# A transformer layer on one core: gate/up as seven block products, tokens in two groups

## The reference

```
n  = rms_norm(x, norm_mix_g)
h  = x + concat(window_attention(n), diff_attention(n)) @ w_out
m  = rms_norm(h, norm_ffn_g)
y  = h + (silu(m @ w_gate) * (m @ w_up)) @ w_down
return rms_norm(y, final_norm_g), keys and values
```

## Time and profile before

| | us |
|---|---|
| runs (3), median | 2766.35 |
| lowest and highest | 2764.15 to 2767.64 |
| span of the profiled execution | 2764.0 |
| TensorE busy | 2640.0 |
| VectorE busy | 1581.0 |
| ScalarE busy | 1136.4 |
| GpSimd busy | 444.8 |
| DMA queues, mean | 48 GB/s |

### The profile page before, as it was taken

One profiled execution on the slowest core, in us unless ns is written; L12 is line 12 of the kernel. 1 busy time (PEld: TensorE's weight loads), 2 busy tenths in 40 slices (PEclk: granted clock), 3 DMA queues, 4 the chain that ended last, 5 costly groups with the idle time before them and its releaser, 6 DMA issues.

```text
span 2764.0 us, 48120 instructions
## 1 busy us (share of the span) xinstructions
PE 2640.0 (96%) x19852; PEld 1645.9 (60%) x19852; DVE 1581.0 (57%) x3263; ACT 1136.4 (41%) x2090; POOL 444.8 (16%) x530
## 2 busy tenths in 40 slices
PE   3999999978899998999999999999999999999998
PEld 1666666656667766555656565656565555656564
DVE  8777776768888773665462525353444444353516
ACT  4566666657889997544211111111120111111113
POOL 1211111105667666000000000000000000000001
PEclk9999999988999999999999999999999999999999
DMA  4123211142210000521101101010101010101003
GB/s 184 54 74 109 93 57 65 46 107 51 40 32 9 9 9 17 190 92 61 54 8 46 31 16 31 16 39 9 39 8 46 1 47 1 46 1 47 1 8 126
DMA packets 119197, 132.95 MB, mean 48 GB/s; under 512 B 42642, under 2 KB 97346, under 8 KB 117954
## 3 DMA queue, kind: packets, MB, share of 16 engines
q1 hardware_dynamic: 118978, 129.87, 14.8%
HBM read 92.20 MB, written 34.84 MB: 46 GB/s over the span
## 4 chain that ended last, share of the span: by engine, by line
PE 58%; DVE 1%; DMA 1%; ACT 0%; issue 0%; POOL 0%; POOLq 0%; ACTq 0%
PE y_ps L2325 6%; PE y_ps L2327 6%; PE y_ps L2326 6%; PE hnT_ps L2312 6%; PE hnT_ps L2313 6%; PE hnT_ps L2314 6%; PE mixT_ps L2312 6%; PE mixT_ps L2313 6%; PE mixT_ps L2314 6%; PE y_ps L2297 2%; PE y_ps L2299 2%; PE y_ps L2298 2%; DMA tail_buffers<-mix_scratch 1%; PE mixT_ps L2274 1%; PE hnT_ps L2284 0%; DVE tail_buffers L2054 0%
## 5 line engine op out<-in xcount | busy, mean ns | idle before, releaser
L2079 DVE SCALAR_TENSOR_TENSOR residual_rows<-y_ps,pair_scales,residual_rows 128x512 f32<-128x512 f32 (+1 forms) x374 | 276.8, 747 | 101.4 <-PE y_ps L2327 100.5
L2312 PE MATMUL hnT_ps<-ffn_inT_hi,tail_buffers 128*128 128x352 f16 x1056 | 330.0, 313 | 0.7 <-ACT ffn_inT_hi L2184 0.7
L2312 PE MATMUL mixT_ps<-ffn_inT_hi,tail_buffers 128*128 128x352 f16 x1056 | 330.1, 313 | 0.0
L2313 PE MATMUL hnT_ps<-ffn_inT_lo,tail_buffers 128*128 128x352 f16 x1056 | 330.0, 313 | 0.0
L2313 PE MATMUL mixT_ps<-ffn_inT_lo,tail_buffers 128*128 128x352 f16 x1056 | 330.0, 313 | 0.0
L2314 PE MATMUL hnT_ps<-ffn_inT_hi,tail_buffers 128*128 128x352 f16 x1056 | 330.0, 313 | 0.0
L2314 PE MATMUL mixT_ps<-ffn_inT_hi,tail_buffers 128*128 128x352 f16 x1056 | 330.0, 313 | 0.0
L2213 ACT ACTIVATE w_out_halves<-mixT_ps,pair_scales 128x352 f32<-128x352 f32 x66 | 36.6, 554 | 706.2 <-PE mixT_ps L2314 706.2
L1094 PE MATMUL z_ps<-w_in_hi_lo,normT_hi 128*128 128x384 f16 x816 | 268.5, 329 | 21.8 <-DVE w_in_hi_lo L681 21.8
L2067 DVE SCALAR_TENSOR_TENSOR w_out_halves<-hnT_ps,pair_scales,w_out_halves 128x352 f32<-128x352 f32 x66 | 38.5, 584 | 432.6 <-ACT w_out_halves L2213 432.6
L2325 PE MATMUL y_ps<-w_out_halves 128*128 128x512 f16 (+1 forms) x748 | 283.8, 379 | 0.0
(11 more groups left out here) (317 smaller groups left out, 5385.0 us busy)
## 6 DMA issues: line engine op xcount, KB each, us to landing
tail_buffers<-in_w_gate SPq DMA_DIRECT2D x11, 1024.0 KB, 5.4
tail_buffers<-in_w_up SPq DMA_DIRECT2D x11, 1024.0 KB, 8.0
tail_buffers<-in_w_down SPq DMA_DIRECT2D x22, 512.0 KB, 3.2
keys_values<-in_w_in SPq DMA_DIRECT2D x8, 1152.0 KB, 16.0
x_tile<-in_x SPq DMA_DIRECT2D x17, 512.0 KB, 3.7
tail_buffers<-mix_scratch SPq DMA_DIRECT2D x17, 512.0 KB, 3.7
residual_rows<-in_x SPq DMA_DIRECT2D x17, 512.0 KB, 4.6
out_y_prompt<-tail_buffers SPq DMA_DIRECT2D x16, 512.0 KB, 2.6
```

The costliest lines, as they stand in the source:

```text
L2079: nc.vector.scalar_tensor_tensor(out, YP[(2 * t + n) % 4][0:rows, :], PS[0:rows, i, F_YI:F_YI + 1], out, ALU.mult, ALU.add).then_inc(h_ok, 1)
L2312: nc.tensor.matmul(out, FH[w][:, k, c], nh, start=k == 0, stop=False)
L2313: nc.tensor.matmul(out, FH[w][:, k, c], nl, start=False, stop=False)
```

## The change

It touches `phase_output_ffn` (and one small transfer in the first stage, a row copy of the norm gain). What it does:

- **Block products.** The gate and up products of a pair are taken as 2 x 2 block products: the width 1024 in two halves of 512, the tokens in two halves. Seven products of blocks and sums of blocks stand for the eight (a scheme of Strassen with sums reused). `PRODUCTS`, `PSUM_OF` and `SLOT_AT` are its tables: which token block or sum a product reads, which PSUM bank it goes to, and where its weight slot lies. Per matrix x (0 gate, 1 up) three banks are used, 0 to 2 and 3 to 5; the down products use 0, 1, 6 and 7. j counts the seven products.
- **Token sums.** The normed rows of two tiles, one of each token half, make four sums (`token_sums`, GpSimd), and 28 chunks in place of 16 are split (`row_hi`, `row_lo`) and transposed (`turn`, in four batches, 56 transposes for two tiles).
- **Weight sums.** GpSimd makes four sums of weight blocks for each pair (`weight_sums`), ScalarE and VectorE split seven slots of 1024 elements (`slot_hi`, `slot_lo`).
- **Sums of products.** ScalarE copies the first product out (`copy_1`), VectorE forms `sum_2`, `sum_3`, `block_22`, `block_21`, `block_12`, and four activations follow in place of two for a block.
- **Two groups of tokens.** The first group has 8 tiles (1024 tokens, halves of 512), the second 9 (1088 tokens, halves of 544, run as 256 and 288 columns). Output tiles 0 to 8 in the order `ORDER`, then 11 pairs, then output tiles 9 to 16, then 11 pairs again. The weight halves made in the first group are stored to DRAM scratch (`store_slot`, `store_down`) and loaded in the second (`slot_back`, `down_back`). Residual rows are kept for 9 tiles and reused.

The core of the diff:

```diff
-NTOK = SEQ + DEC
-TB = 6
-TBW = NTOK // TB
+ORDER = (0, 4, 1, 5, 2, 6, 3, 7, 16, 8, 12, 9, 13, 10, 14, 11, 15)
+Q0 = 9
+HALF = (4 * P, 4 * P + DEC // 2)
+STEPS = 14
+PRODUCTS = (B11, B21, T2, T1, T3, T4, B22)
+PSUM_OF = (0, 0, 1, 2, 1, 1, 2)
...
 GpSimd
+                def token_sums(u):
...
+                    nc.gpsimd.tensor_tensor(part(0), NF[1][:, half[0]], NF[0][:, half[0]], ALU.subtract).then_inc(t_ok, 1)
+                    nc.gpsimd.tensor_tensor(part(2), NF[1][:, half[1]], NF[1][:, half[0]], ALU.subtract).then_inc(t_ok, 1)
...
+                def weight_sums(i):
...
+                    pool.wait_ge(gw_lo, 7 * i)
+                    nc.gpsimd.tensor_tensor(XS[0], quad(0, 0), quad(1, 0), ALU.subtract).then_inc(ws_ok, 1)
+                    pool.wait_ge(ws_ok, 4 * i + 1)
+                    nc.gpsimd.tensor_tensor(quad(1, 0), quad(1, 0), quad(1, 1), ALU.add).then_inc(ws_ok, 1)
...
+                for i in range(PAIRS):
+                    if i + 1 < PAIRS:
+                        max_gate_up(i + 1)
+                        weight_sums(i + 1)
                     max_down(i)
...
 VectorE, a pair of the first group
+                    product_act(0, i, i, 512, 0)
...
+                    if more and i:
+                        max_gate_up(i + 1, 0)
+                    sum_2(0, i, 512, 0)
+                    sum_2(0, i, 512, 1)
+                    act_lo(0, 0, i, 512, 0)
+                    if more:
+                        if i == 0:
+                            max_gate_up(i + 1, 0)
+                        max_gate_up(i + 1, 1)
+                    max_down(i)
+                    if more:
+                        gate_up_scales(i + 1)
+                    down_scales(i)
+                    if more:
+                        slot_lo(i + 1, 0)
+                    sum_3(0, i, 512, 0)
+                    block_22(0, i, 512, 0)
...
 TensorE
+                def before_product(e, i, b, n, j, x):
...
+                    if j == 1:
+                        pe.wait_ge(cp_ok, 2 * n + x + 1)
+                    if j == 4:
+                        pe.wait_ge(u2_ok, 2 * n + x + 1)
+                    if j == 5:
+                        pe.wait_ge(u3_ok, 2 * n + x + 1)
+                    if j == 6:
+                        pe.wait_ge(c22_ok, 2 * n + x + 1)
...
+                    for k in range(4):
+                        nh, nl = (NV[e][h][:, 4 * o + k, at:at + w] for h in range(2))
+                        wh, wl = (slot(j, h)[:, 4 * x + k, :] for h in range(2))
+                        nc.tensor.matmul(out, wh, nh, start=first and k == 0, stop=False, skip_group_check=True)
+                        nc.tensor.matmul(out, wh, nl, start=False, stop=False, skip_group_check=True)
+                        last = nc.tensor.matmul(out, wl, nh, start=False, stop=k == 3, skip_group_check=True)
+                    last.then_inc(gu_ok, 1)
```

More of the change, by code:

```diff
@@ L1923, in _ @@
+                for n in range(9):
+                    sp.wait_ge(stored[n], 16 if n == 8 else 32)
             @block.gpsimd
@@ new lines, in act_lo @@
+                def act_lo(e, b, n, w, m):
+                    dve.wait_ge(ah_ok, 4 * n + m + 1)
+                    f, h = (0, 1, 1, 0)[m], (0, 1, 0, 1)[m]
+                    gate = (SI(e, w), U3(e, 0, w), P1(e, 0, w), U2(e, 0, w))[m]
+                    for a, z, c in a_parts(e, b, h):
+                        v = slice(c, c + z - a)
+                        last = nc.vector.tensor_tensor(AL[e][:, f, v], gate[:, a:z], AH[e][:, f, v], ALU.subtract)
+                    last.then_inc(al_ok, 1)
@@ L2077, in add @@
+                def add(e, i, y):
+                    t = tiles(e)[y // 2]
                     rows = P if t < NT else DEC
-                    out = hrow(t)[0:rows, half[n]]
-                    nc.vector.scalar_tensor_tensor(out, YP[(2 * t + n) % 4][0:rows, :], PS[0:rows, i, F_YI:F_YI + 1], out,
+                    dve.wait_ge(y_ok, y_base(e, i) + y + 1)
+                    out = hrow(t)[0:rows, half[y % 2]]
+                    nc.vector.scalar_tensor_tensor(out, BK[y_bank(e, y)][0:rows, :], PS[0:rows, i, F_YI:F_YI + 1], out,
@@ L2097, in _ @@
                     out_weight_lo(k)
[L2098 to L2118 removed]
+                gain_scale()
@@ new lines, in _ @@
+                    sum_3(0, i, 512, 0)
+                    block_22(0, i, 512, 0)
+                    sum_3(0, i, 512, 1)
+                    block_22(0, i, 512, 1)
+                    if more:
+                        slot_lo(i + 1, 1)
+                    product_act(0, i, i, 512, 1)
+                    block_21(0, i, 512, 0)
+                    act_lo(0, 0, i, 512, 1)
+                    block_21(0, i, 512, 1)
+                    product_act(0, i, i, 512, 2)
+                    down_lo(i, 0)
@@ new lines, in _ @@
+                    block_12(0, i, 512, 0)
+                    act_lo(0, 0, i, 512, 2)
+                    down_lo(i, 1)
+                    block_12(0, i, 512, 1)
+                    product_act(0, i, i, 512, 3)
+                    act_lo(0, 0, i, 512, 3)
+                    if not more:
+                        norm_row(Q0 - 1)
+                        mix_lo(Q0)
+                    for y in range(16):
+                        add(0, i, y)
+                        if more and y in (1, 3, 6, 9, 12):
+                            slot_lo(i + 1, 2 + (1, 3, 6, 9, 12).index(y))
+                        if not more and y == 11:
+                            mixT_lo_out(Q0)
+                        if not more and y % 2 and y // 2 >= NORM_BEHIND:
+                            scale_row_tile(y // 2 - NORM_BEHIND)
@@ L2328, in down @@
+                        nc.tensor.matmul(out, ah, DL[:, f, half[y % 2]], start=False, stop=False)
+                        last = nc.tensor.matmul(out, al, DH[:, f, half[y % 2]], start=False, stop=f == 1)
                     last.then_inc(y_ok, 1)
@@ new lines, in _ @@
+                for q in range(Q0, NTT):
+                    output_tile(q)
+                for i in range(PAIRS):
+                    for b in range(2):
+                        n = block_no(1, i, b)
+                        for j in range(7):
+                            for x in range(2):
+                                gate_up(1, i, b, n, j, x)
+                                if i == 0 and b == 0 and (j, x) in ((1, 1), (5, 1), (6, 0), (6, 1)):
+                                    turn(8, ((1, 1), (5, 1), (6, 0), (6, 1)).index((j, x)))
+                    pe.wait_ge(d_back, 32 * (i + 1))
+                    if i == 0:
+                        pe.wait_ge(n_hi, 36)
+                        pe.wait_ge(n_lo, 36)
+                    for y in range(18):
+                        if y in (0, 8):
+                            pe.wait_ge(al_ok, 4 * block_no(1, i, 1) + (4 if y else 3))
+                        down(1, i, y)
```

1079 lines of the change are left out of this document (713 added, 366 removed).

## The result

The changed kernel takes **2975.3 us** (median of 4 runs, 2975.2 to 2976.2) against 2767.0 us of the kernel before (median of 4 runs made beside it): ratio 1.075, 95% interval 1.074 to 1.077. It is 208 us slower, as forecast (2974 us).

What follows compares the result with a forecast made beforehand. TensorE's column count was taken as the bound (busy 96% of 2764.0 us). Terms -121 + 13 + 214 + 38 + 56 + 8 = +208 us gave 2972, with 2.35 for the median 2974 us; range 2880 to 3070.

Steps and rivals of the forecast that it cites:

- The bound: Whole kernel: TensorE's column count is the time; other engines matter only once they make it wait.
- Part 1: Gate/up products: fewer columns, 75.1 us a pair in place of 86.1, -121 us for 11 pairs.
- part 2: Token rows: 504 transposes in place of 272, +13 us.
- Part 3: First group, pairs 1 to 9: TensorE's sixth product waits 21.1 us for sum_3, plus 2.3 for clock; +214 us.
- Part 4: First pair: pair 1's weight loads late, so the same chain delays TensorE 35.7 us plus 2.3 for clock; +38 us.
- Part 5: Output tiles: TensorE's transposes wait for token sums and their split, 7.9 us seven times; +56 us.
- Part 6: Second group: 3 us for its pairs and 5 us for the turn between the groups; +8 us.
- Code changes for nothing: Rival: GpSimd's switches between reduction and arithmetic cost nothing, TensorE waits 8 us a pair; 2844 us, 8 in 100.
- GpSimd held off by VectorE: Rival: each of the four weight sums loses 3 us to VectorE, a pair 12 more; 3094 us, 5 in 100.
- The covered wait: Rival: second reduction done by 21.3 us in a pair, so TensorE never stops; 2692 us, 5 in 100.

Runs made afterwards that it cites:

- c2_all_together: c1_down_first with token-sum transposes half a tile later and, in the first pair too, the down weight prepared before the next gate/up weight: 2738.1 us, ratio 0.991.
- a4_sums_cut: Changed kernel with GpSimd's four weight sums cut to an eighth of their width, order of all engines kept: 2898.6 us.
- a1_sums_last: Changed kernel with GpSimd's four weight sums of the next pair moved behind its second reduction (maxima of the down weight): 2837.2 us.
- b0_before_code_change: Kernel before the change with one tiny GpSimd addition put between the two reductions of each pair: 2763.1 us against 2768.9 beside it.
- c1_down_first: a1_sums_last with the down weight's whole preparation moved to the start of pairs 1 to 9 of the first group: 2765.3 us.
- p1_sums_cut_and_last: a1_sums_last with the four weight sums cut to an eighth of their width: 2789.2 us.

## Why the prediction was right, point by point

**The bound** holds: where TensorE isn't made to wait, it runs at the time of its columns, in all runs.

**Part 1** (columns, -121) and **part 2** (transposes, +13): second-group pairs of 62.45 us are the columns of my sum (38.8 + 23.3 = 62.1) and 0.3 more, and first-group pairs come to 58.1 in c2_all_together (57.0 by columns).

**Part 3** (+214): nine pairs at 80.3 against 57.0 are +210. Step by step: wait 21.1 forecast and 20.8 found; four sums 9.6 and 9.6; code changes 7.1 and 5.9 forecast, 7.1 and 5.85 found; clock 2.3 forecast, 2.1 found on average. One reading in it was off: before, the first of the two reductions was used 26.3 us after it was made (1501.41 to 1527.68) and not 28 or more, which changes nothing. a4_sums_cut and a1_sums_last show that these pieces are causes: take 7.6 us of sums out and 7.7 a pair go; let the second reduction not stand behind them and the wait falls to 2.6.

**Part 4** (+38): about 37. The wait was 30.4 and not 35.7 us, but TensorE came to it later than forecast, 32.1 us into the pair and not 27.6: it had already waited 2.45 us for a second weight half, `slot_lo` (1271.46), at half clock behind. The chain itself (reduction 34.6 us in, sixth product 62.5) is the forecast one (35.6 and 63.2).

**Part 5** (+56) is the term that was mis-sized. The norm factor of every second row on GpSimd's timeline, of before and then of after, gives the time of two output tiles:

```profile
1164.26 0.55 POOL L1933 TENSOR_TENSOR h_stats<-h_stats 128x1 f32<-128x1 f32 x1
...
1188.56 0.55 POOL L1933 TENSOR_TENSOR h_stats<-h_stats 128x1 f32<-128x1 f32 x1
```
```profile
1175.29 0.55 POOL L2077 TENSOR_TENSOR h_stats<-h_stats 128x1 f32<-128x1 f32 x1
...
1207.05 0.55 POOL L2077 TENSOR_TENSOR h_stats<-h_stats 128x1 f32<-128x1 f32 x1
```

24.3 us became 31.8, so 7.5 more, of which 1.3 are the 24 transposes of part 2: 6.2 a unit where I had 7.9, some 43 us for seven. The wait itself was 3.9 and not 5 (8.0 once, ahead of the first pair).

**Part 6** (+8) was too small, by more than part 5 had too much. What parts 1 to 4 leave of the measured +209.5 is some 70 us for parts 5 and 6 together (64 forecast), so about 27 for part 6: 4 in the pairs of the second group (0.3 us each, as forecast, though in the short products themselves and in no wait) and 23 for the turn between the groups and the tiles next to it, where I had 5. The waits there: 8.0 for the last batch ahead of the first pair, 2.7 at 2137.5 and 7.6 at 2165.1 for the first tiles of the second group, 3.0 in its first pair, with half clock behind. I had priced the turn by its loads and stores, and not by TensorE's first tiles on both sides of it. These two errors, and the small ones of parts 3 and 4, cancel to the 1 us between forecast and result, so its exactness is partly luck; the three main terms are not. The bounds of the terms add up to 2897 and 3079, and not to 2890 and 3070; the result is far from either.

**The rivals.** Code changes for nothing: excluded by b0_before_code_change (6.7 us with no other cause) and a4_sums_cut; but it is true where GpSimd waits anyway. GpSimd held off by VectorE: no part of the weight sums, since VectorE stood still while they ran, as the clock of part 3 had it. Of the four token sums of a unit only the second ran beside a residue of VectorE and took 1.7 in place of 1.3 us. a1_sums_last shows that the interference becomes real, 5 us a pair, as soon as the stall is taken away. It was not a rival to the forecast but the next limit behind it. The covered wait: its condition was wrong. In a1_sums_last the second reduction ends 21.9 us into the pair (1361.83, the pair from 1339.9), 0.6 past the 21.3 that was to be enough, and TensorE waits 2.6 us, since VectorE has its two maxima and the gate/up scales in front of `down_scales` until 24.3. It needed VectorE past `down_scales` in time, which c1_down_first brings about. 2692 was then too hopeful: in c2_all_together the first pair is 25 us longer than the others and each other is 1.2 above its columns, and for the 30 us that the forecast of 2692 takes off besides the two waits it gives no working.

## What to carry to other kernels

A scheme that saves columns on the busiest engine hands its additions to others, and their order, not their sum, decides: with the same 48132 instructions the time was 2975 or 2738 us. For each new wait, follow the waiting engine's order back until an engine is found that has work of its own in front, and put the step that others wait for ahead of the step that nobody needs yet. When the stall is out, look for what now runs side by side that never did before.

## What the runs showed of the hardware

- GpSimd's change between arithmetic and reductions costs time only where the next instruction is due. From arithmetic to a reduction it is 5.6 to 6.3 us when the reduction is due at once (a4_sums_cut, the changed kernel), and the reduction starts 0.14 us behind its operand when 24.7 us of waiting lie ahead (b0_before_code_change). From a reduction to arithmetic it is 6.6 to 7.4 us when the arithmetic is due (the same runs), and 0.08 us behind the operand after 141 us of waiting (the kernel before). So the change seems to be made before the instruction's wait is fulfilled. That it is a load of code is a name for the gap; no row shows what is done in it.
- VectorE and GpSimd at once: 0.75 became 2.83 and 0.68 became 2.08 us on VectorE for operands in SBUF only, 2.34 became 2.7 to 3.2 on GpSimd, and VectorE's 0.68 with an operand in a bank stayed (a1_sums_last, p1_sums_cut_and_last). Both sides pay, and VectorE the more. In the ten pairs of a1_sums_last each of VectorE's 30 slowed instructions of this width ends 0.55 us behind the end of the sum beside it.
- Behind waits of one length, 20.3 to 21.1 us, TensorE ran at 0.50 for anything from 2.8 to 5.7 us (the changed kernel). What sets this length is open here.
